# One fused two-block network on one core: the order of work around the last mLSTM head, and the last gate block by token halves

## What is computed

```python
# mLSTM, head h (of 4, width 128), per query token
num = weights(q, k, gates) @ v ;  den = sum(weights)
h   = num / maximum(|den|, exp(-m))
hm  = rms_norm(h, gain) * sigmoid(mo)              # the output gate
# NSA, compressed branch: 31 compressed keys, 8 heads
s_c = q @ Kc - slope * distance ;  p_c = softmax(where(valid, s_c, NEG))
# the end of the network
gate = sigmoid(rms_norm(x) @ w_gate)               # 8 blocks of 128 channels
x    = x + gate * (p @ w_proj)
return rms_norm(x, final_g)
```

## Time and profile before

| what | value |
|---|---|
| median of 3 runs | 1432.68 us (1432.66 to 1433.53) |
| the profiled execution's own time | 1434.12 us |
| its span in the trace | 1431.9 us |
| PE busy | 97% of the span |
| DVE, ACT, POOL busy | 59%, 46%, 38% |
| mean granted TensorE clock | 0.989 of full |

### The profile page before, as it was taken

The page is one execution under the profiler, slowest core; times in us unless marked ns, Lnnn a source line. Parts: engine busy times, 40 slices in busy tenths (PEclk is TensorE's granted clock), DMA queues, the critical chain, the costliest instruction groups (busy, mean ns, idle before and its releaser), DMA issues.

```text
span 1431.9 us, 18136 instructions
## 1 busy us (share of the span) xinstructions
PE 1386.2 (97%) x6768; PEld 1095.0 (76%) x6768; DVE 838.8 (59%) x1435; ACT 652.8 (46%) x1108; POOL 537.0 (38%) x288
## 2 busy tenths in 40 slices
PE   8999999999999999989999999999999999999997
PEld 6777878777778878757888887675667888888886
DVE  5576464757567744784676322357756655544754
ACT  6644524535455543684555312335555323223553
POOL 2543554634320034465000333325354555555200
PEclk9999999999999999999999999989999999999998
DMA  5222212222233222211223342131002333333331
GB/s 185 89 74 60 89 60 88 74 59 74 73 90 89 88 88 89 60 60 40 94 88 118 103 132 74 31 103 31 16 28 79 101 90 102 98 94 103 104 89 59
DMA packets 33078, 116.82 MB, mean 82 GB/s; under 512 B 3932, under 2 KB 4316, under 8 KB 32736
## 3 DMA queue, kind: packets, MB, share of 16 engines
q1 hardware_dynamic: 31976, 111.85, 25.5%
q10 hardware_dynamic: 1016, 3.81, 0.8%
HBM read 113.55 MB, written 2.10 MB: 81 GB/s over the span
## 4 chain that ended last, share of the span: by engine, by line
PE 86%; DVE 4%; ACT 4%; issue 2%; POOL 2%; DMA 1%; ACTq 0%; DVEq 0%; POOLq 0%
PE bank L1244 83%; PE bank L1671 1%; PE bank L1514 1%; ACT wsh L847 1%; DMA h<-in_xT 1%; POOL wsl L691 1%; DVE arena L1827 0%; PE bank L1387 0%; POOL arena L749 0%; PE bank L1421 0%; ACT arena L1180 0%; ACT arena L908 0%; DVE arena L2187 0%; DVE arena L2240 0%; POOL arena L756 0%
## 5 line engine op out<-in xcount | busy, mean ns | idle before, releaser
L691 POOL TENSOR_TENSOR wsl<-ring,wsh 128x1024 fp32r<-128x1024 f32 x145 | 352.3, 2430 | 575.4 <-ACT wsh L847 575.3
L847 ACT ACTIVATE wsh<-ring 128x1024 fp32r<-128x1024 f32 x199 | 210.6, 1058 | 505.0 <-PE bank L1244 482.5
L1244 PE MATMUL bank<-parts1h,wsh 128*128 128x512 f32 x728 | 292.2, 401 | 8.6 <-DVE parts1l L1752 2.7
L1244 PE MATMUL bank<-parts0h,wsh 128*128 128x512 f32 x704 | 282.4, 401 | 3.8 <-issue 1.3
L1244 PE MATMUL bank<-parts1l,wsh 128*128 128x512 f32 x728 | 285.2, 392 | 0.0
L1244 PE MATMUL bank<-parts1h,wsl 128*128 128x512 f32 x728 | 285.1, 392 | 0.0
L1244 PE MATMUL bank<-parts0h,wsl 128*128 128x512 f32 x704 | 274.6, 390 | 0.0
L1244 PE MATMUL bank<-parts0l,wsh 128*128 128x512 f32 x704 | 274.4, 390 | 0.0
L1244 PEld LDWEIGHTS bank<-parts1h,wsh 128*128 128x128 f32 x728 | 137.7, 189 | 44.8 <-issue 4.7
L1244 PE MATMUL bank<-arena 128*64 128x128 f32 (+9 forms) x964 | 152.2, 380 | 11.4 <-DVE arena L2240 3.7
L1244 PEld LDWEIGHTS bank<-parts0h,wsh 128*128 128x128 f32 x704 | 132.3, 188 | 38.4 <-issue 6.8
(11 more groups left out here) (305 smaller groups left out, 1840.1 us busy)
## 6 DMA issues: line engine op xcount, KB each, us to landing
ring<-in_wstream SPq DMA_DIRECT2D x206, 512.0 KB, 3.6
arena<-in_alibi ACTq DMA_DIRECT2D x2, 1024.0 KB, 5.0
outT<-arena SPq DMA_DIRECT2D x8, 256.0 KB, 2.8
h<-in_xT SPq DMA_DIRECT2D x2, 256.0 KB, 5.7
h<-in_xT ACTq DMA_DIRECT2D x2, 256.0 KB, 6.5
h<-in_xT SPq DMA_DIRECT2D x1, 512.0 KB, 8.5
h<-in_xT ACTq DMA_DIRECT2D x1, 512.0 KB, 9.7
arena<-in_cmpb ACTq DMA_DIRECT2D x1, 496.0 KB
```

The costliest lines, as they stand in the source:

```text
L691: return nc.gpsimd.tensor_tensor(dst, src, hi.bitcast(F32), ALU.subtract)
L847: nc.scalar.activation(wsh[n % NSET][:, :], src, ACT.Copy).then_inc(*done("high", ("high", L)))
L1244: return nc.tensor.matmul(*args, **kw)
```

## The change

It changes the order of the list at two places, and cuts the last gate block in two.

1. The compressed scores `nsa[:2]` stand in front of the filling `mo` 1 and `("mB", 3)`.
2. Behind `mB` 3 come the compressed exponentials and factors, then the first `nS` of branch s, then the matmuls of `mo` 2 as filling, then `mfac`, then the rest of `mo` 2. `mo` 3 is the first step of `between`, and `mg` 0 to 3 are each one place later.
3. In `mg`, DVE writes the next diagonal behind the norm, not ahead of it.
4. The last gate block `("ple", 2, 7)` becomes `("tail", 0)` and `("tail", 1)`, each for 256 tokens: 24 matmuls of 256 columns into a bank of its own, and half-wide operations behind it.
5. The final sums, root, reciprocal and results run in two parts of two token tiles each. `turn` 1 comes behind the sums of the first part and takes tiles 4, 5 and 6, and of tile 7 the first two token tiles.

```diff
-    for h, x in enumerate([("ak", 0), ("ak", 1), ("mo", 0), ("mo", 1)]):
-        out += [("F", *x), ("mB", h), x]
-
     seq = [...]
     nsa = pipeline("n", seq, [x for x in seq if x[1:] == (1, "w")])
-    out += nsa[:2] + [("mfac",)] + nsa[2:7] + [("mo", 2)]
-    between = {0: [("mg", 0)], 1: [("mo", 3)], 2: [("mg", 1)], 3: [("mg", 2)], 4: [("mg", 3)]}
+    for h, x in enumerate([("ak", 0), ("ak", 1), ("mo", 0), ("mo", 1)]):
+        out += (nsa[:2] if h == 3 else []) + [("F", *x), ("mB", h), x]
+    out += nsa[3:7] + nsa[2:3] + [("F", "mo", 2), ("mfac",), ("mo", 2)]
+    between = {0: [("mo", 3)], 1: [("mg", 0)], 2: [("mg", 1)], 3: [("mg", 2)], 4: [("mg", 3)]}
...
-    out += [("ple", 2, m) for m in range(5)] + [("turn", 0), ("ple", 2, 5), ("ple", 2, 6), ("turn", 1), ("ple", 2, 7)]
-    out += [("norm", 7), ("last",)]
+    out += [("ple", 2, m) for m in range(5)] + [("turn", 0), ("ple", 2, 5), ("ple", 2, 6)]
+    out += [("tail", 0), ("tail", 1), ("norm", 7), ("turn", 1), ("last",)]
...
 # ScalarE
+                if step == ("tail", 0):
+                    square(7, KD - 2)
+                if k == "tail":
+                    act.wait_ge(*at("gscaled", 2, KD - 1, a[0]))
+                    nc.scalar.activation(part, part, ACT.Sigmoid).then_inc(...)
+                    if a[0]:
+                        link(nc.scalar.activation(tiny[:, :], eps[:, :], ACT.Sqrt))
+                if step == ("norm", 7):
+                    final_root(0)
                 if k == "last":
-                    act.wait_ge(*at("rinv"))
                     for t in range(NT):
+                        if t == 2:
+                            final_root(1)
+                        if t % 2 == 0:
+                            act.wait_ge(*at("rinv", t // 2))
...
 # TensorE
+                if k == "tail":
+                    b = open_bank(step)
+                    w = weights(("ple_gate", 2, KD - 1))
+                    c = slice(256 * a[0], 256 * a[0] + 256)
+                    for kt in range(KD):
+                        last = mm3(b[:, 0:256], [q[:, tok(kt)] for q in w], [q[:, kt, c] for q in hn], kt == 0, kt == KD - 1)
...
                 if step == ("norm", 7):
-                    turned(1, 6)
+                    pe.wait_ge(*at("ssadd", 7, KD - 2))
+                    for part in range(2):
+                        b = open_acc(("ss", 7, part))
+                        for t in range(2 * part, 2 * part + 2):
+                            mm(b[:, t:t + 1], ssacc[:, tok(t)], ones[:, 0:1], start=t % 2 == 0, stop=False, ...)
+                    final_sums(0)
...
                 if k == "last":
-                    turned(1, 7)
+                    final_sums(1)
+                    pe.wait_ge(*at("h", 7, KD - 1, 1))
+                    turned(1, KD - 1, range(2, NT))
...
 # VectorE
+                if k == "tail":
+                    m, c = KD - 1, slice(256 * a[0], 256 * a[0] + 256)
+                    gb = gsig[m % 2][:, c]
+                    if a[0] == 0:
+                        ssadd(7, m - 1)
+                        ...
+                    dve.wait_ge(*at("mm", *step))
+                    nc.vector.tensor_tensor(gb, ps(step)[:, 0:256], rtb[:, c], ALU.mult)...
+                    dve.wait_ge(*at("gsig", 2, m, a[0]))
+                    link(nc.vector.tensor_tensor(gb, gb, pp[2][:, m, c], ALU.mult))
+                    nc.vector.tensor_tensor(h[:, m, c], h[:, m, c], gb, ALU.add)...
+                    dve.wait_ge(*at("h", 7, m, a[0]))
+                    nc.vector.tensor_tensor(sq[:, (KD * 7 + m) % 3, c], h[:, m, c], h[:, m, c], ALU.mult)...
...
                 if k == "mg":
                     h_ = a[0]
-                    if h_ + 1 < M_HEADS:
-                        mdiagonal(h_ + 1)
                     dve.wait_ge(*at("hm", h_))
                     dve.wait_ge(*at("mm", *step))
                     nc.vector.scalar_tensor_tensor(hm[:, h_, :], hm[:, h_, :], ...)
+                    if h_ + 1 < M_HEADS:
+                        mdiagonal(h_ + 1)
```

More of the change, by code:

```diff
@@ L294, in jobs_of @@
         return [(k, *a[:-1], t) for t in range(NT)] if a[-1] == 0 else []
+    if k == "tail":
+        return [step]
     if k == "turn":
@@ L338, in accs_of @@
     if k == "norm":
[L339 removed]
+        return [("ss", a[0])] if a[0] < 7 else [("ss", 7, 0), ("ss", 7, 1)]
     if k == "nb":
@@ L867, in _, with final_root @@
                             .then_inc(*done("final_act", ("turned", t), ("free", "fin", t, 0)))
+                if step == ("tail", 0):
+                    square(7, KD - 2)
+                if k == "tail":
+                    act.wait_ge(*at("gscaled", 2, KD - 1, a[0]))
+                    part = gsig[(KD - 1) % 2][:, 256 * a[0]:256 * a[0] + 256]
+                    nc.scalar.activation(part, part, ACT.Sigmoid).then_inc(*done("gsig", ("gsig", 2, KD - 1, a[0])))
+                    if a[0]:
+                        link(nc.scalar.activation(tiny[:, :], eps[:, :], ACT.Sqrt))
+                def final_root(part):
+                    act.wait_ge(*at("mm", "ss", 7, part))
+                    c = slice(2 * part, 2 * part + 2)
+                    nc.scalar.activation(nrm[:, 0, c], acc(("ss", 7, part))[:, c], ACT.Sqrt, bias=eps[:, 0:1], scale=1.0 / D)\
+                        .then_inc(*done("rms", ("rms", 7, part)))
+                if step == ("norm", 7):
+                    final_root(0)
                 if k == "last":
-                    act.wait_ge(*at("rinv"))
                     for t in range(NT):
+                        if t == 2:
+                            final_root(1)
+                        if t % 2 == 0:
+                            act.wait_ge(*at("rinv", t // 2))
                         act.wait_ge(*at("mm", "fin", t, 1))
@@ L876, in _ @@
                     link(nc.scalar.activation(tiny[:, :], eps[:, :], ACT.Sqrt))
-                if k == "norm":
+                if k == "norm" and a[0] < 7:
                     act.wait_ge(*at("mm", "ss", a[0]))
@@ L1004, in _ @@
                         square(2 * i + 2, m)
-                    if m == KD - 1 and i == 2:
-                        link(nc.scalar.activation(tiny[:, :], eps[:, :], ACT.Sqrt))
                 if k == "sines":
@@ L1315, in _, with turned @@
                 k, a = step[0], step[1:]
-                def turned(half, m):
-                    pe.wait_ge(*at("h", 7, m))
-                    for t in range(NT):
+                def turned(half, m, tokens=range(NT)):
+                    if m < KD - 1:
+                        pe.wait_ge(*at("h", 7, m))
+                    for t in tokens:
                         last = mm(ps(("fin", t, half))[:, tok(m - 4 * half)], h[:, m, tok(t)], wdiag[:, m, :], start=True, stop=True)
@@ L1327, in _, with final_sums @@
                         open_bank(("fin", t, a[0]))
-                    for m in ((0, 1, 2, 3), (4, 5))[a[0]]:
+                    for m in ((0, 1, 2, 3), (4, 5, 6))[a[0]]:
                         turned(a[0], m)
-                if step == ("norm", 7):
-                    turned(1, 6)
-                if k == "norm":
+                    if a[0]:
+                        pe.wait_ge(*at("h", 7, KD - 1, 0))
+                        turned(1, KD - 1, range(2))
+                def final_sums(part):
+                    pe.wait_ge(*at("sq", 7, KD - 1, part))
+                    for t in range(2 * part, 2 * part + 2):
+                        last = mm(acc(("ss", 7, part))[:, t:t + 1], sq[:, (KD * 7 + KD - 1) % 3, tok(t)], ones[:, 0:1],
+                                  start=False, stop=True, skip_group_check=True)
+                    last.then_inc(*done("mm", ("mm", "ss", 7, part)))
+                if k == "tail":
+                    b = open_bank(step)
[3 more added lines that the diff above has]
+                        last = mm3(b[:, 0:256], [q[:, tok(kt)] for q in w], [q[:, kt, c] for q in hn], kt == 0, kt == KD - 1)
+                    if a[0]:
+                        last.then_inc(*used(("ple_gate", 2, KD - 1), ("mm", *step)))
+                    else:
+                        last.then_inc(*done("mm", ("mm", *step)))
+                if step == ("norm", 7):
+                    pe.wait_ge(*at("ssadd", 7, KD - 2))
+                    for part in range(2):
+                        b = open_acc(("ss", 7, part))
+                        for t in range(2 * part, 2 * part + 2):
+                            mm(b[:, t:t + 1], ssacc[:, tok(t)], ones[:, 0:1], start=t % 2 == 0, stop=False, skip_group_check=True)
+                    final_sums(0)
+                elif k == "norm":
                     if a[0] == 0:
@@ L1766, in _ @@
                     ver = a[0]
+                    if ver == 7:
+                        continue
                     dve.wait_ge(*at("rms", ver))
-                    if ver == 7:
-                        nc.vector.reciprocal(nrm[:, 1, :], nrm[:, 0, :]).then_inc(*done("final_dve", ("rinv",)))
-                        continue
```

(5 more changed lines are left out.)

17 lines of the change are left out of this document (11 added, 6 removed).

## The result

The changed kernel takes 1437.43 us (median of 8 runs, 1435.1 to 1439.15) where the kernel before takes 1432.77 (8 runs, 1431.98 to 1436.79). The ratio is 1.003, with a 95% interval of 1.0022 to 1.0039: some 4.3 us slower, where the prediction had +1.5 as likeliest and +4.7 as its upper end. The profiled execution took 1435.1 us for a span of 1432.9, the lowest of the eight. Its span is only 1.0 us above that of the kernel before, because it is 2.3 us ahead at 913 us, where no edit has come yet.

The account below looks back on a forecast made before the run. PE, busy 97% of the span, was taken as the bound, so gains could come only from its waits, half clock and the end. Middle +4.6 and end -3.1 made +1.5 us, 1434.2 against the median 1432.68; range 1429.4 to 1437.4.

Parts of the forecast that it names:

- the forecast's own range: Whole kernel: the likeliest case, 1432.0 to 1436.9 us, with the middle at +2.4 to +7; chance 0.60.
- rival C: Last gate block: weight loads pace the half blocks at 0.189 us, the end gains only 0.6; 1436.7 us, chance 0.13.
- Rival B: Middle: comes out even, by clock kept up or the extra unit made up later; 1429.6 down to 1428.0, chance 0.25.
- D: Last gate block: weight load and stream add up for each matmul; 1444 us, chance 0.02.
- Compressed scores, then `mo` 1's bank: Ahead of `mo` 1: early scores gain about 1 us, then PE stands from 930.0 to 934.0 for a bank L2240 frees.
- Clock in `mo` 1: In `mo` 1, behind the bank wait: 1.6 us lost to low clock, bounds 0 and 2.7.
- Head 3 and four scores: Between `mo` 1 and `mo` 2: head 3 takes 3.9 us and the four scores of branch s 0.9.
- Clock in `mo` 2: In `mo` 2: loses the same 1.5 us of clock as before, bounds 0 to 1.7.
- `mo` 3 waits for the means: Ahead of `mo` 3: PE waits 2.3 us for the chain of the means, its bank freed by L2173.
- Clock in `mo` 3: In `mo` 3: again loses 1.7 us of clock, ending at 965.25 against 965.04.
- One unit more behind `mo` 3: Behind `mo` 3: head 0's unit starts only there, the next factors come at 973.6; +4.6 us, bounds +1.0 and +6.5.
- The end: Last block and outputs: halves at 0.12 us per matmul, squares and transfers sooner; 3.1 us gained, bounds -3.4 and -0.6.

Follow-up runs that it names:

- e2: Kernel before with only the middle of the change (new list order), its end left as before; 1440.99 us, ratio 1.0048.
- e1: Kernel before with only the end of the change (half blocks, two-part outputs), its middle left as before; 1429.83 us, ratio 0.9971.
- e11: The end alone once more, same code as e1, run beside other kernels; 1429.21 us, ratio 0.9974.
- e3b: Changed kernel with the two compressed score tiles of token tile 0 sharing one bank; 1434.19 us, ratio 1.0009.
- e5: Changed kernel with DVE masking the early compressed scores only behind head 3; 1444.29 us, ratio 1.0077.
- e6: Changed kernel with both the shared bank for the compressed scores and `mg` 0 ahead of `mo` 3; 1430.96 us, ratio 0.9988.
- e4: Changed kernel with `mg` 0 ahead of `mo` 3 again, as before the change; 1434.44 us, ratio 1.0006.
- e8: Changed kernel with DVE writing the next head's diagonal ahead of the norm again; 1438.38 us, ratio 1.0035.
- e9: Changed kernel with one unused 512-column fp32 matmul ahead of each of `mg` 1, 2 and 3; 1439.42 us, ratio 1.0044.
- e7: The end alone (e1) plus the early compressed scores sharing a bank, means, fillings and norms in the old order; 1431.47 us, ratio 0.9986.
- e10: The end alone (e1) with two unused 512-column fp32 matmuls filling PE's wait ahead of `mo` 3; 1430.88 us, ratio 0.9991.

## Why the prediction came out as it did

The sign of the likeliest case was right and its size was too small. The range held only at its edge: its top is 1437.4, the median is 1437.43, and 1437.0 by the ratio, above the forecast's own range (up to 1436.9). The top of the range was there for rival C too, whose 1436.7 is near and whose cause is absent, so that the range held is partly luck. In the clock of the profiles, the middle was to cost 4.6 us and costs 6.0; the end was to gain 3.1 and gains 3.0. By the ratios the middle costs 6.9 (e2) and the end gains 4.2 and 3.7 (e1, e11), all with intervals of over 1 us to either side. Rival B (the middle even) fell: the bank wait and the late unit are both there. Rivals C and D fell with the row at 1415.17. D's 1444 was also 2 us too high by its own terms (48 x 0.107 = 5.1 us above C's 1436.7), and the middle's upper bound stands as +6.5 in one place and +7 in another; neither moves the forecast. Step by step:

- **Compressed scores, then `mo` 1's bank.** Predicted: PE idle 4 us, released by L2240, `mo` 1 starting 15.0 us behind the end of (`ak`, 1). Measured: 3.66 us, by that line (now L2308), with `mo` 1 starting 14.93 us behind. e3b and e5 show both halves of the cause, the rotation and the masks in DVE's queue.
- **Clock in `mo` 1.** 1.6 us predicted, 1.8 measured; e3b shows that it is lost there without the wait too, and e6 (5.61) that it need not be.
- **Head 3 and four scores.** 4.85 predicted, 4.77 measured.
- **Clock in `mo` 2.** "loses the same 1.5 us of clock": wrong, it ran at full clock, 5.57 us, here and in the six other kernels with this order and no wait ahead of it (e2, e3b, e4, e6, e8, e9: 5.56 to 5.60). A gain of 1.4 us that I left out.
- **`mo` 3 waits for the means.** 2.3 us by L2173 predicted; 2.44 by the same line (L2241) measured. The chain of `mfac` took 2.86 us, exactly as in the earlier trace rows.
- **Clock in `mo` 3.** 1.7 predicted, 2.2 measured. Up to the end of `mo` 3 I had 46.3 us from (`ak`, 1), and it was 45.6.
- **One unit more behind `mo` 3: the step that was mis-sized.** From the end of `mo` 3 to `wo` the prediction makes it 24.0 us, and it was 26.12; these 2.1 us, less the 0.7 that the steps above came short, are the 1.4 by which the middle was off. The factors were to come 8.35 us behind `mo` 3's end, and came 9.03 behind (970.28 - 961.25): 0.7 more, of which 0.3 lies between the block's end and DVE's scaling at 961.51, 0.5 in the first unit, where L2386 took 1.35 us ahead of the factors, and 0.2 in the diagonal (e8 has 8.81), while the other links came some 0.2 to 0.3 shorter than I took them. Set in the prediction's clock (3.3 us later) these factors stand at 973.6, just as forecast, but by luck: the 0.7 gained before and the 0.7 lost here cancel. Then "the units after that are the same as before and go on from there": from these factors to `wo` it took 17.09 us, against 15.67 before (984.66 - 968.99), 1.4 more. Of this 1.0 is PE at half clock (16.11 in e9) and 0.4 the diagonals of two heads, 0.2 each (e8). So the units were not the same as before: the forecast put both terms at nothing.
- **What undoing the late unit gives.** `mg` 0 ahead of `mo` 3 gives 3.0 to 3.4 us in the times and 0.5 (e4) to 2.1 us (e6 against e3b) outside the blocks, not 4.6, since it waits for the same chain. I had counted the delay as a cost of the unit's place alone; a part of it belongs to the place of `mfac`.
- **A place that the prediction did not look at.** At 1095 us all kernels wait 1.80 to 1.82 us for DVE (`parts1l`), ahead of the same matmuls. The changed kernel then ran at half clock and lost 1.4 us against the kernel before:

```profile
1098.35 0.79 PE L1268 MATMUL bank<-parts1h,wsh 128*128 128x512 f32 x1 [1.81 <-DVE parts1l L1842]
1098.94 0.63 PE L1268 MATMUL bank<-parts1l,wsh 128*128 128x512 f32 x1
```

  No edit touches this place. Over the starts of the weight copies on ACT, the changed kernel stands 2.3 us ahead of the kernel before at 913, 2.7 behind at 1073 and 4.1 behind at 1111: 5.0 for the middle up to there and 1.4 here.
- **The end.** The squares of the second half are done at 1424.0, in the old clock 1420.0, where 1420.15 was predicted; the transfers take 7.7 us from the first issue to the end of the span, where 7.25 was taken and 7 to 7.5 was the sign. Predicted -3.1, measured -3.0. The matmuls of 256 columns stand 0.12 apart, as taken. The Trainium skill ("TensorE: Matmul & The Clock Gate", The mechanism) has two sentences on this: a weight load overlaps with matmuls in flight only where the row group differs, and a load into the background weight buffer is pulled ahead too. The row contradicts the first and fits the second; to which buffer a load goes, no run here shows. The table load took 1.28 us, and the next instruction stands 0.01 us behind it (1422.65 and 1423.94). A drain of 1.38 us ahead of or behind the load, as the Trainium skill has it ("ScalarE: Activation LUTs", What ACT_TABLE_LOAD costs), is not in this trace.

What stays open: why the clock falls in one execution and not in another of the same code. It blurs the sum: the middle costs 6.5 us in the profiles from 913 on (5.0, and 1.4 at 1095), or 7.4 with the 0.9 that (`ak`, 1) had won, and 6.9 to 8.5 in the ratios, where e2's interval alone reaches from 5.0 to 8.7. Whether the loss at 1095 belongs to the middle is not shown. e6 and e7 are no faster than e1 in the medians although their profiles have the shorter middle (63.81 and 65.00 against 65.67 and 64.68); with one profile of each, this can't be settled.

## What to carry to other kernels

Before moving a job forward in a hand-written order, count the rotation of its buffers: it shifts the buffer of every later job, and the one that the next big block gets may be freed by the engine whose queue the moved job has just lengthened (3.6 us here). A chain that was hidden by a block on the other engine is paid once it stands behind that block: the means behind `mo` 2, with the `mg` steps a place later, saved 3.8 us ahead and cost 7.1 behind, and with `mg` 0 back in its place the way to `mo` 3 was still 3.8 us longer (5.57 in e7, 9.33 in e6). And measure the parts of a change apart: the half that made this one slower hid a half that gains 0.3% by itself. Last, an order of two operations that looks neutral can change how long they take: the diagonal behind the norm cost 0.2 us a head.

## What the runs showed of the hardware that was not expected

- The same code at the same place loses clock in one execution and not in another. Behind the same wait of 1.80 us at 1095, the kernel before, e1, e3b, e4, e6 and e10 lost nothing there, the changed kernel, e2, e5 and e7 lost 1.4 to 1.6 us, and e8, e9 and e11 lost 3.2. Even ahead of the edit, at 172 us, where the code is the same, the profiles of the changed kernel and of the kernel before are 2.6 us apart. The runs of e11 spread from 1427.57 to 1431.12.
- A half clock on PE costs little where another engine sets the pace: 5 us of it were worth 1.0 (e9). In the linear blocks it is paid in full: 5.57 or up to 8.2 us.
- A small operation on DVE can take many times its usual time: L2386, 128x4, took 0.17, 0.78, 1.35 and 1.16 us in four units in a row. The three long ones end 0.02 to 0.03 us behind the end of an operation that GpSimd was in: DVE at 955.05, 965.01 and 969.60, POOL at 955.03, 964.99 and 969.57. The same holds for every operation of this line over 0.3 us between 900 and 1075, five here and five (as L2318) in the kernel before; one short one (0.17 at 1046.51) ran while GpSimd was busy, so GpSimd's work does not always hold it. No experiment isolates the cause. Timelines of DVE and POOL, changed kernel:

```profile
954.27 0.78 DVE L2386 TENSOR_SCALAR small<-small 128x4 f32<-128x4 f32 x1
...
963.66 1.35 DVE L2386 TENSOR_SCALAR small<-small 128x4 f32<-128x4 f32 x1
...
968.44 1.16 DVE L2386 TENSOR_SCALAR small<-small 128x4 f32<-128x4 f32 x1
...
952.60 2.43 POOL L696 TENSOR_TENSOR wsl<-ring,wsh 128x1024 fp32r<-128x1024 f32 x1 [10.47 <-ACT wsh L852]
...
962.64 2.35 POOL L696 TENSOR_TENSOR wsl<-ring,wsh 128x1024 fp32r<-128x1024 f32 x1 [4.63 <-ACT wsh L852]
...
968.30 1.27 POOL L696 TENSOR_TENSOR parts0l<-arena,parts0h 128x512 fp32r<-128x512 f32 x1 [1.89 <-ACT parts0h L1193]
```

- Two orders on DVE divide the same delay differently. With the diagonal behind the norm, L2331 took 1.07 us and GpSimd's product beside it (L785) 1.04; with it ahead (e8), L2331 took 0.69 and the product 1.42.
